# Two-block recurrent model: values and second keys moved to the other half of the partitions, one direction's straight products beside the other's crossing ones

## The reference

```
def wkv_scan(state0, r, decay, kk, b, v, k, reverse):
    def step(S, inp):
        r_t, w_t, kk_t, b_t, v_t, k_t = inp
        sa = jnp.einsum("bhvk,bhk->bhv", S, kk_t)
        S = (S * w_t[:, :, None, :] - sa[..., None] * b_t[:, :, None, :]
             + v_t[..., None] * k_t[:, :, None, :])
        return S, jnp.einsum("bhvk,bhk->bhv", S, r_t)
```

## Time and profile before

| | us |
|---|---|
| median of 3 runs | 1715.99 |
| lowest, highest | 1715.91, 1730.39 |
| profiled execution, its own time | 1721.18 |
| span of the profiled execution | 1719.4 |
| TensorE busy in the span | 1604.4 (93%) |
| VectorE busy | 916.6 (53%) |
| ScalarE busy | 541.7 (32%) |
| GpSimd busy | 208.4 (12%) |
| mean granted TensorE clock | 0.937 |

### The profile page before, as it was taken

One profiled execution on the slowest core, in us unless ns is written; L12 is line 12 of the kernel. 1 busy time (PEld: TensorE's weight loads), 2 busy tenths in 40 slices (PEclk: granted clock), 3 DMA queues, 4 the chain that ended last, 5 costly groups with the idle time before them and its releaser, 6 DMA issues.

```text
span 1719.4 us, 36464 instructions
## 1 busy us (share of the span) xinstructions
PE 1604.4 (93%) x15540; PEld 1355.4 (79%) x15540; DVE 916.6 (53%) x1465; ACT 541.7 (32%) x890; POOL 208.4 (12%) x206
## 2 busy tenths in 40 slices
PE   7899998999999969999998999999958999999997
PEld 4787976999999857778877888778747788888886
DVE  1624214565667545788887223676443455556222
ACT  3422233212121223444433223545543322223221
POOL 0000002223233001111111111000001111111011
PEclk8899997878999988999999998999969999999998
DMA  8232101212110112222222222222001222222221
GB/s 328 74 142 74 61 14 51 101 52 101 53 53 4 52 50 74 74 98 89 84 96 92 95 90 90 79 76 74 25 25 51 97 98 94 91 93 89 101 101 66
DMA packets 33885, 139.73 MB, mean 81 GB/s; under 512 B 2272, under 2 KB 2784, under 8 KB 33248
## 3 DMA queue, kind: packets, MB, share of 16 engines
q1 hardware_dynamic: 33616, 135.76, 22.3%
q10 hardware_dynamic: 144, 2.10, 0.3%
HBM read 135.75 MB, written 2.10 MB: 80 GB/s over the span
## 4 chain that ended last, share of the span: by engine, by line
PE 81%; DVE 11%; ACT 4%; issue 3%; DMA 0%; POOL 0%; DVEq 0%; ACTq 0%; SPq 0%
PE bank L621 53%; PE bank L754 12%; DVE ffn_sb L2433 4%; PE bank L631 2%; DVE w_up L2039 1%; PE bank L941 1%; ACT w_up L1370 1%; PE bank L584 1%; PE bank L1255 1%; PE bank L860 1%; PE bank L882 1%; PE bank L1244 1%; PE bank L862 1%; PE bank L566 1%; PE bank L884 1%
## 5 line engine op out<-in xcount | busy, mean ns | idle before, releaser
L621 PE MATMUL bank<-hf_hi,w_up 128*128 128x512 f32 x1376 | 426.2, 391 | 0.0
L621 PEld LDWEIGHTS bank<-hf_hi,w_up 128*128 128x128 f32 x1376 | 259.9, 189 | 53.7
L621 PE MATMUL bank<-hf_lo,w_up 128*128 128x512 f32 x688 | 271.8, 395 | 5.5 <-DVE w_up L2039 4.7
L621 PE MATMUL bank<-act_hi,w_down 128*128 128x512 f32 x704 | 218.5, 392 | 0.0
L754 PE MATMUL bank<-arena 64*64 64x32 f32 (+2 forms) x4992 | 195.4, 239 | 18.1 <-POOL arena L1882 6.9
L754 PEld LDWEIGHTS bank<-arena 64*64 64x64 f32 x4992 | 189.2, 151 | 22.4 <-issue 14.6
L2039 DVE TENSOR_TENSOR w_up<-ring,w_up 128x1024 fp32r<-128x1024 f32 x88 | 108.1, 1229 | 105.8 <-ACT w_up L1370 105.7
L1370 ACT ACTIVATE w_up<-ring 128x1024 fp32r<-128x1024 f32 x88 | 93.0, 1058 | 217.4 <-PE bank L621 217.4
L621 PEld LDWEIGHTS bank<-hf_lo,w_up 128*128 128x128 f32 x688 | 130.0, 189 | 39.6 <-DVE w_up L2039 13.3
L621 PEld LDWEIGHTS bank<-act_hi,w_down 128*128 128x128 f32 x704 | 133.4, 189 | 27.9
L2433 DVE SCALAR_TENSOR_TENSOR ffn_sb<-ffn_sb 128x512 f32<-128x512 f32 x176 | 151.5, 861 | 6.3 <-ACT ffn_sb L1611 0.8
(11 more groups left out here) (318 smaller groups left out, 2373.4 us busy)
## 6 DMA issues: line engine op xcount, KB each, us to landing
ring<-w SPq DMA_DIRECT2D x92, 1024.0 KB, 4.7
ring<-w SPq DMA_DIRECT2D x32, 704.0 KB, 4.0
arena<-w SPq DMA_DIRECT2D x2, 3072.0 KB, 22.4
x<-xT SPq DMA_DIRECT2D x1, 2048.0 KB, 11.6
arena<-w SPq DMA_DIRECT2D x2, 1024.0 KB, 19.2
x<-xT ACTq DMA_DIRECT2D x1, 2048.0 KB, 9.0
outT<-x SPq DMA_DIRECT2D x4, 512.0 KB, 2.7
arena<-ctxT SPq DMA_DIRECT2D x1, 1024.0 KB, 7.2
```

Of the source, the lines that this page charges most:

```text
L621: ins = mm(out, w[:, a, k, :], of_block(b, k0 + k), start=first and k == 0 and m == 0, stop=last and k == n - 1 and m == 2)
```

## The change

The values (`v_tok`), the masked second scores (`kr`) and the turned second keys (`tok`, part 1) are now kept in the opposite half of the partitions. The matmuls that make them have their inputs in one half and their output in the other (`crossed_tiles`); so have the products that use them, whose result comes back to the half of its head. A crossing product uses the two corners of the array that a straight one leaves free.

`state_in`, `turned`, `state_terms` and `results` no longer take a direction but a part. Part 0 alternates direction 0's straight products with direction 1's crossing ones, part 1 the other way round. Each result is now summed over both parts, so its bank is complete only after part 1. Part 1 waits on a new semaphore until part 0's matmuls have ended (`state_half`, `turned_half`, `terms_half`, `results_half`). The third product of `results` is a part 2, straight for one direction after the other. The order of TensorE changes with it: the updates come after dx 2 and ada_parts, part 1 of the state products stands between nx 2 and dx 2, the parts of `turned` and `state_terms` alternate, and the parts of the results stand before nx 4, before dx 4 and before nx 5. On VectorE only `second_result` moves, behind level 4.

```diff
+        CROSSED = ((HALVES[0], HALVES[1]), (HALVES[1], HALVES[0]))
...
+            def crossed_tiles(out, lhs, rhs):
+
+                for j in range(NJ):
+                    for r, o in CROSSED:
+                        last = mm(out(j, o), lhs(j, r), rhs(j, r), start=True, stop=True)
                 return last
...
-            def state_terms(n, d):
-
-                sc = scans[d]
-                done("gu", d, 2 * n + 2)
-                done("tok", d, n + 1)
-                v_in = v_tok[:, place(d, n) // L]
+            def state_terms(n, part):
+
+                if part == 0:
+                    for d in both:
+                        done("gu", d, 2 * n + 2)
+                        done("tok", d, n + 1)
+                else:
+                    pe.wait_ge(s["terms_half"], 2 * n + 2)
+                straight, across = part, 1 - part
+                sc, other = scans[straight], scans[across]
+                v_in = v_tok[:, place(across, n) // L]
                 for j in range(NJ):
-                    out = bank[d][3][:, L * j:L * j + L]
+                    at = slice(L * j, L * j + L)
                     for r in HALVES:
-                        mm(out[r], sc.tok[r, 0, j, :], sc.gu[r, j, :], start=True, stop=False)
+                        a = mm(bank[straight][3][r, at], sc.tok[r, 0, j, :], sc.gu[r, j, :],
+                               start=part == 0 and j == 0, stop=part == 1 and j == NJ - 1)
+                    for r, o in CROSSED:
+                        b = mm(bank[across][3][o, at], other.tok[r, 1, j, :], v_in[r, j, :],
+                               start=part == 0 and j == 0, stop=part == 1 and j == NJ - 1)
+                a.then_inc(s[f"ds_mm{straight}" if part else "terms_half"], 1)
+                b.then_inc(s[f"ds_mm{across}" if part else "terms_half"], 1)
...
+            def results(n, part):
...
+                if part == 2:
+                    for d, sc in enumerate(scans):
+                        for j in range(NJ):
+                            for r in HALVES:
+                                last = mm(bank[d][0][r, L * j:L * j + L], sc.gu[r, j, :],
+                                          sc.nr[r, n % 2, j, L:2 * L], start=False, stop=j == NJ - 1)
+                        last.then_inc(s[f"y_mm{d}"], 1)
+                    return
```

More of the change, by code:

```diff
@@ L879, in state_terms @@
                 for j in range(NJ):
-                    out = bank[d][3][:, L * j:L * j + L]
+                    at = slice(L * j, L * j + L)
                     for r in HALVES:
-                        mm(out[r], sc.tok[r, 0, j, :], sc.gu[r, j, :], start=True, stop=False)
-                    for r in HALVES:
[L884 to L902, removed]
@@ new lines, in results @@
+            def results(n, part):
+                at_half = 4 * (n - NCC) + 2 * part
+                if part == 0:
+                    for d in both:
+                        done("gu", d, 2 * n + 2)
+                        done("nr", d, min(n + 2, NC))
+                        pe.wait_ge(s[("ada_row", "mod")[d]], (8, 1)[d] + min(n + 2, 8))
+                else:
+                    pe.wait_ge(s["results_half"], at_half)
+                if part == 2:
+                    for d, sc in enumerate(scans):
+                        for j in range(NJ):
+                            for r in HALVES:
[3 more added lines that the diff above has]
+                    return
+                straight, across = part, 1 - part
+                sc, other = scans[straight], scans[across]
+                v_in = v_tok[:, place(across, n) // L]
+                for j in range(NJ):
+                    at = slice(L * j, L * j + L)
+                    for r in HALVES:
+                        a = mm(bank[straight][0][r, at], sc.S[r, n % 2, j, :], sc.ktrt[r, n % 3, j, L:2 * L],
+                               start=part == 0 and j == 0, stop=False)
+                    for r, o in CROSSED:
+                        b = mm(bank[across][0][o, at], v_in[r, j, :], other.kr[r, n % 2, j, L:2 * L],
+                               start=part == 0 and j == 0, stop=False)
+                a.then_inc(s["results_half"], 1)
+                b.then_inc(s["results_half"], 1)
@@ L966, in _ @@
                 if n >= 0:
-                    for d in both:
-                        updates(n, d)
+                    state_in(n, 1)
                 if inv:
@@ L973, in _ @@
                     ada_parts(n)
+                if n >= 0:
+                    for d in both:
+                        updates(n, d)
+                if 0 <= m < NC - 1:
+                    turned(m, 0)
                 if 0 <= n < NC - 1:
[L975 to L976 removed]
+                    state_terms(n, 0)
                 if 0 <= m < NC - 1:
[L978 to L979 removed]
+                    turned(m, 1)
+                if 0 <= n < NC - 1:
+                    state_terms(n, 1)
                 if inv:
@@ L988, in _ @@
                 if n >= NCC:
-                    for d in both:
-                        results(n, d)
+                    results(n, 0)
                 if inv:
@@ L2277, in _ @@
                         x_turned(m, d, 4)
+                if n >= NCC + NCX // 2:
+                    for d in both:
+                        second_result(n, d)
+                if inv:
                     for d in both:
```

73 lines of the change are left out of this document (48 added, 25 removed).

## The result

The changed kernel takes 1730.89 us (median of 20 runs, 1724.65 to 1746.48), the kernel before 1718.63 in the runs beside it: a ratio of 1.0079, with a 95% interval from 1.0056 to 1.0102. The forecast was 1730, "slower, but within 1%". The profiled execution of after has a span of 1737.7 us, 18.3 above that of before. By the medians the loss is 12.3, so its rows show more than the usual loss.

The account below looks back on a forecast made before the run. TensorE, busy 93% of the span, bounds the kernel before; with packing VectorE becomes the chain. Step changes sum to +14.5 us on 1721.18, so 1735.7; the median lies 5.2 lower, so 1730, range 1688 to 1757.

Parts of the forecast that it names:

- The packing term: Small matmuls of the recurrence: four corners take 58 ns a round, 39 us less TensorE work over 42 groups.
- no packing: Rival for the packed matmuls: four corners take 116 ns a round, +48 us, so 1764; chance 0.15.
- VectorE has become the chain: Step 7: VectorE's state, masks and keys after late terms delay TensorE; 22.9 us at full clock against 23.06.
- The second wait: In each step, TensorE stalls 2.4 us before nx of level 4, waiting for VectorE's keys and x.
- The clock step: TensorE's clock falls in every step, also 7 to 10; step 7 takes 27.6 us, 4.6 more than before.
- Moved waits: nothing: Updates placed after dx of level 2 and the modulation products delay VectorE, ScalarE and GpSimd at no cost.
- -1.5 a step: Steps 0 to 3: earlier nx of level 4 gains 1.5 us each, -6 for the four.
- one such pause, partly hidden: Steps 0 and 1: a TensorE pause partly hidden behind VectorE's chain, within the gain taken for these steps.
- the 39 us: TensorE work that packing removes from 42 groups of 32 calls in steps 0 to 11.

Follow-up runs that it names:

- c_dve: Changed kernel with VectorE reordered: state operations split behind the masks of levels 3 and 4, keys behind x of level 4; ratio 1.0014 to the kernel before.
- d_fill: Changed kernel with unused matmuls added in VectorE's two waits of every step, ten before dx of level 3, fourteen before nx of level 4; ratio 1.0119.
- a_straight: Changed kernel's order and waits, but values and second keys stay in their own half, so every product is straight; ratio 1.0125 to the kernel before.
- i_unpacked: Changed kernel's swapped halves, with products, waits and VectorE's work in the order of the kernel before, no interleaving; ratio 0.9972, 1712.73 us.
- e_small_after: Changed kernel with the modulation weights' ring loads cut from 1024 to 32 KB, part of the computation left out; ratio 1.0017, 1719.03 us.
- g_both: Packing in the order of the kernel before, plus VectorE's state operations split and moved later and keys behind level 4; ratio 1.0045.
- b_order: Changed kernel's packing, but in the order of the kernel before, for TensorE and VectorE; ratio 1.0010 to the kernel before.

## Why the prediction came out right, step by step

**In the total it was right (1730 against 1730.9), in good part by luck: errors of opposite sign.** The forecast was 14.0 us above a median of 3 runs, 1715.99; over 20 runs the kernel before took 1718.63, and the loss was 12.3. Forecast and found in the profile: steps 0 to 3 -6 and +4.4; 4 to 6 +4.3 and +3.7; step 7 +4.6 and +3.5; 8 and 9 +7.8 and +3.2; 10 and 11 +4.4 and +8.8. Together, with -0.6 for step -1, 14.5 and 23.6, of which 5.3 came back outside the recurrence. In steps 10 and 11 the forecast took step 11 at full clock; from 596.90 to the end at 618.13 the clock was 0.60 on average.

**The packing term: right.** A round of four records, one in each corner, costs 58 ns or a little more: 64 records in about 0.95 us, 15 ns a record instead of 29. The rival "no packing" falls. The Trainium skill's rule (TensorE: Matmul & The Clock Gate, Part 3, "The mechanism"), that a weight load overlaps running matmuls only when its row group differs, is not borne out for these tiles, two and two of which share rows: this case's records disagree with it.

**"VectorE has become the chain": right in kind, its terms mis-sized.** Step 7 from its start at 508.15: the state begins at 8.5 (forecast 6.03), takes 2.1 (1.81; one operation on SBUF of 0.42 took 0.81 beside GpSimd), dx of level 3 starts at 10.9 (8.16), the keys take 2.5 (3.18), nx of level 4 starts at 13.8 (12.0). Of the 2.5 at the head, 1.1 is an issue pause in the turned tiles, 1.1 had collected ahead of the terms. c_dve shows the chain's price: 11 us by the ratios. The second wait, 2.4 us before nx of level 4, did not come as forecast. In step 7 no row shows it: at half clock dx and the half of the results filled the 2.8 us from 519.08 to 521.92, where the forecast had 1.4 us of work. In the whole recurrence such waits (L2242) make 1.4 us, in two pieces.

**The clock step: right that it falls, its price mis-sized.** It falls in every one of steps 7 to 9. The forecast price was too high: from nx of level 4 to the end of step 7 it is 534.68 - 521.92 = 12.8 us, not 15.6, and steps 7 to 9 took 26.5, 24.4 and 26.3, not 27.6. I had put the two later parts of the results on top at the lower level; that they stand in waits that were there in any case is my reading, not shown by a run. (Their sum had a slip too: twice 0.47 and 0.93 is 2.80, not 0.86 + 1.71.) d_fill shows the cause of the falls: with work in the waits the clock stays.

**"Moved waits: nothing" was wrong.** a_straight, which has the moved waits and nothing packed, is 21 us slower than before. How much of it is each wait was not tried.

**The step that failed: "-1.5 a step" for steps 0 to 3**, with pauses taken over from before. In steps 0 to 5 the longest of each step came to 2.2 to 4.1 us, where before has 1.3 to 2.0 in steps 0, 1 and 3. In steps 0 to 3 the issue pauses add up to 14.1 us instead of 5.2, and that is most of the 10 us by which the sum missed there. It was visible ahead of time: the trace of before has the rows quoted above, in steps 0, 1 and 3. I had not put them among my rows (the earlier trace rows has only waits for VectorE), and the forecast speaks of one such pause, partly hidden, without a price of its own.

**Where the 39 us went.** Packing in the same order yields 8 us, with the wide margin given above. 17.5 us became issue pauses (27.0 against 9.5 in a_straight). The rest is not settled to the microsecond: half clock rose from 96 to 128 us, which at half the rate is up to 16 us, but it overlaps with the waits for VectorE.

**What is shown of the issue pauses, and what stays argued.** That TensorE waits in them for its own instructions is shown by the packets in the traces, next section. That it gets there sooner because the packed stream runs faster fits all the runs (issue is 27 to 31 us in the kernels packed throughout with full loads, 8.6 to 13.7 in those packed nowhere), but no kernel was tried with a shorter program.

## What to carry to other kernels

Before you pay for shorter matmuls in a stage, look for pauses that end with "issue" in it: a stream that is twice as fast may hand its gain back in more and longer ones. Two groups that use different corners of the array overlap where they meet without interleaving. The layout without the new order was the one complete version here that beat before (0.9972, and its interval ends at 0.9998). When a change removes work from an engine, follow what the next engine's order makes late, and test order and work apart.

## What the runs showed of the hardware

The long issue pauses lie at fixed distances in instructions. From one to the next, in before, in after twice, and in i_unpacked (by stretch; the first x is TensorE's records):

```profile
316.44:341.44 25.00, 23.02 (x630) 22.63 (x630) 12.54 (x38) 5.30 (x15) 5.08 (x8) 0.81 0.23 85
```

```profile
317.13:342.87 25.74, 20.57 (x628) 19.77 (x628) 13.32 (x38) 4.97 (x15) 4.47 (x7) 0.77 0.24 85
342.87:371.88 29.01, 25.28 (x626) 24.72 (x627) 13.39 (x41) 3.89 (x13) 2.85 (x4) 0.68 0.21 73
```

```profile
314.76:339.97 25.21, 22.28 (x629) 21.59 (x629) 12.75 (x38) 5.20 (x15) 4.71 (x7) 0.80 0.24 85
```

Here it is some 628 records, with other lines of the kernel behind each. It is not always that number: from 371.88 to 404.64 in after it is 755, from 459.77 to 494.18 879. All these are near multiples of 126 (5, 6 and 7 times). The page of after has a queue that fits, 1.70 MB in 104 packets, 16 KB each:

```profile
q8 instruction: 104, 1.70, 0.4%
```

In the recurrence 63 of its packets stand against some 7900 TensorE records: one for every 126. The traces hold the time of each packet, and it settles what the pauses wait for:

| kernel | pause ends | its length | packet starts | packet lands | from landing to the end |
|---|---|---|---|---|---|
| before | 341.44 | 1.98 | 339.00 | 339.93 | 1.51 |
| after | 342.87 | 4.13 | 340.41 | 341.37 | 1.50 |
| after | 404.64 | 3.61 | 402.30 | 403.32 | 1.32 |
| i_unpacked | 394.14 | 3.11 | 391.66 | 392.65 | 1.49 |
| e_small_after | 479.17 | 1.75 | 476.66 | 477.78 | 1.39 |

The fourteen kernels have 84 issue pauses of 0.9 us or more between 300 and 612 us. Every one ends 1.18 to 1.66 us after an instruction packet has landed; of 101 waits over 0.5 us that a semaphore ended, 21 do. A packet takes 0.9 to 1.6 us in all kernels, so a long pause comes from a packet that starts late: in the two rows of after it starts 1.7 and 1.3 us after TensorE has stopped. The row of 0.6 at the end of the recurrence (L1020 in before) follows no landing and is of another kind.

In all, the pauses cost 1.6 and 4.1 us in the unpacked streams without large transfers, 8.6 to 13.7 in unpacked streams beside ring loads, and 27 to 31 where the stream is packed throughout as well. Single ones reach 3.1 us in the kernels packed nowhere and 4.7 in the packed ones (g_both).

A product of 64x64 in the second pair of corners runs beside one in the first although they share rows. And the clock fell at 518.40, in step 7, where pauses of 1.1 and 1.6 us stand among short matmuls, most of them of 32 columns, while before it had stayed at 1.00 with one of 0.66. Length alone does not tell: in b_order it stayed at 1.00 with a pause of 1.38 us before 539.04.
